# A two-block transformer forward pass: HGRN level products of two blocks at once, and a rearranged start

## The chip, the cores and the metric

The kernel runs on one core of a Trainium2 chip. The metric is the device time of one execution in microseconds (us), the median of several runs. Engines: TensorE (PE for its matmuls, PEld for its weight loads), VectorE (DVE), ScalarE (ACT), GpSimd (POOL) and SyncE (SP, which here only issues DMAs). They run side by side and meet at semaphores. Each takes its own instructions in order.

## The reference

One sequence of 512 tokens of width 1024 goes through two layers, in float32. The first has gated linear attention, dilated attention and a squared-relu MLP. The second has stick-breaking attention, an HGRN2 mixer and a gated MLP. The part of the HGRN mixer that the change touches:

```python
def hgrn2_mixer(q_in, f_in, i_in, g_in, lb, norm_g):
    f = lb + (1.0 - lb) * jax.nn.sigmoid(f_in)
    log_f = jnp.log(f)
    key = 1.0 - f
    q = jax.nn.silu(q_in)
    val = i_in
    ...
        b = jnp.cumsum(gc, axis=2)
        diff = b[:, :, :, None, :] - b[:, :, None, :, :]
        decay = jnp.exp(jnp.where(mask, diff, -jnp.inf))
        attn = jnp.einsum('bhtk,bhsk,bhtsk->bhts', qc, kc, decay)
        o_intra = jnp.einsum('bhts,bhsv->bhtv', attn, vc)
    ...
    o = rms_norm(o, norm_g)
    return o * jax.nn.silu(g_in)
```

And the first step of the first layer:

```python
nx = rmsnorm(h, attn_norm_g[l])
proj = jnp.einsum('bsd,dp->bsp', nx, w_in[l])
```

## The kernel before

**Products of activations with weights.** Activations lie transposed (features on the 128 partitions, 512 tokens along the row). Every weight matrix is cut into units of 8 k-steps by 256 columns, and a unit into pieces of at most 1024 columns. SP brings a piece to `RAW` (three buffers), ACT rounds it to its high part `WH` (five buffers), and its low part `WL` is the difference. For pieces 2 to 7 POOL makes `WL` (L1682), for pieces 0 and 1 DVE (L1093), and from piece 8 on (`ADDED`) ACT writes the negated high part (L734) and POOL issues a DMA that adds the weights to it (L1678). Activations have a high and a low part too (`NH`, `NL`), so every k-step of a tile is three matmuls of 512 columns: high by high (L432), low activation (L434), low weight (L436). The normalisation's factor is applied after the product, so the first products need only x times the norm's weights (`gains`): row k of `NH` on ACT (L707), of `NL` on DVE (L1098). The squares, their sum `acc` and the mean (L449, fp32, 512 columns) run beside them.

**The order.** Every engine's program is a merge of streams. Each stream yields a due time, and `merge` always takes the earliest. The unit of time is one k-step of a full tile, three matmuls. `T_H` is where the last projection of the second layer, `gs` (16 tiles), begins, and `h_time(i)` places task i of HGRN at `T_H + 0.1 + 3 (i + 2)`: three k-steps between two tasks.

**HGRN.** A head's 512 tokens are four blocks of 128. The causal products inside a block are done by levels, m = 1, 2, 4, ... 64: at level m the first half of each pair of stretches of m tokens holds keys, the second half queries. There are 8 tasks in each of 4 heads: task 0 is the diagonal (L605), tasks 1 to 7 the levels (L612). For a level:

1. DVE takes differences of cumulative log gates into `hD` (L1511, and L1513 for m under 64).
2. ACT takes the exponential (L960, or L946 and L948 for m = 64).
3. DVE multiplies with keys and queries into `hX` (L1493 and L1494, 256 elements each).
4. TensorE makes four products, one a block: a block's 128 columns of `hX` are the weights, its 64 query columns stream.
5. DVE stores the allowed entries into `ATh` with a mask (`keep_level`, L1285; the diagonal at L1543).

Two pairs of buffers (`hD`, `hX`) alternate. Blocks further apart have their own products of `x128` and `x256` (L620, L626). At the end of a head `sum_values` (L544) multiplies `ATh` with the values `vH`, and the result's mean of squares is a product with a matrix of 1/128 (L639).

DVE and ACT also serve the gates' products in this stage: the scaling out of PSUM (L1576) and the sigmoid (L675, L677, L679 on ACT, L683 on DVE, L687 on ACT).

## Time and profile before

| | us |
|---|---|
| median of 3 runs | 1421.49 |
| lowest and highest | 1420.95 and 1422.03 |
| the profiled execution's own time | 1421.15 |
| its span in the trace | 1419.9 |

| engine | busy, us | share of the span |
|---|---|---|
| PE | 1392.8 | 98% |
| PEld | 1129.2 | 80% |
| ACT | 864.4 | 61% |
| DVE | 619.5 | 44% |
| POOL | 203.3 | 14% |

Stages can be found by their lines. The first two tiles run from 7 to 23 us. The HGRN tasks run from 834 to 944 us. A matmul's busy time includes the drain of its pipeline, so its start to the next start tells the rate. An fp32 product appears as two rows of PE, one a pass. A timeline row with an "idle before" part names how long the engine stood and what ended that.

### The profile page before, as it was taken

How to read it: one execution, taken by the hardware profiler on the slowest of the kernel's cores; microseconds unless marked ns; L12 is line 12 of the kernel's file. 1: busy time of each engine (PE TensorE's matmuls, PEld its weight loads, DVE VectorE, ACT ScalarE, POOL GpSimd, SP SyncE). 2: the span in 40 equal slices, each digit the busy share in tenths (PEclk: the TensorE clock that was granted, in tenths of full speed). 3: DMA queues.
4: the chain of work that ended last, by engine and by line, in shares of the span. 5: the costliest groups of instructions: out<-in, count | busy, mean ns of one | idle time of the engine just before them, and what ended most of it. 6: DMA issues, size and time to landing. Idle time of an engine off the chain costs nothing.

```text
span 1419.9 us, 17692 instructions
## 1 busy us (share of the span) xinstructions
PE 1392.8 (98%) x6886; PEld 1129.2 (80%) x6886; DVE 619.5 (44%) x1177; ACT 864.4 (61%) x1267; POOL 203.3 (14%) x231
## 2 busy tenths in 40 slices
PE   7999999999999999999989999999999999999999
PEld 5977966788888888887867778887788888888887
DVE  5054466521211212357578778955534322341232
ACT  5574575654644535666678778676556644663562
POOL 3210000111111111111100011011111111111110
PEclk9999999999999999999999999999999999999999
DMA  6976543698888888877744566669988888888875
GB/s 216 240 166 144 142 114 90 153 209 192 193 191 199 194 188 198 191 169 169 166 109 105 119 144 149 162 149 267 223 200 188 196 188 199 190 194 192 195 168 125
DMA packets 72935, 247.93 MB, mean 175 GB/s; under 512 B 8242, under 2 KB 8258, under 8 KB 72724
## 3 DMA queue, kind: packets, MB, share of 16 engines
q0 software_dynamic: 31536, 113.54, 46.8%
q1 hardware_dynamic: 40452, 131.67, 27.7%
q10 hardware_dynamic: 864, 1.60, 0.3%
q8 instruction: 54, 0.88, 0.2%
q14 instruction: 29, 0.24, 0.1%
HBM read 240.45 MB, written 6.32 MB: 174 GB/s over the span
## 4 chain that ended last, share of the span: by engine, by line
PE 84%; ACT 7%; DVE 5%; issue 2%; DMA 2%; POOL 0%; DVEq 0%; ACTq 0%; POOLq 0%
PE bank L432 25%; PE bank L436 25%; PE bank L434 25%; PE bank L612 2%; ACT WH L726 1%; PE bank L544 1%; ACT WL L734 1%; DVE eb L1352 1%; DMA WL<-in_w_in 1%; ACT eb L880 1%; PE bank L563 1%; PE bank L587 1%; DMA RAW<-in_w_in 1%; PE bank L577 1%; DVE eb L1348 1%
## 5 line engine op out<-in xcount | busy, mean ns | idle before, releaser
L432 PE MATMUL bank<-NH,WH 128*128 128x512 f32 x1152 | 468.3, 407 | 8.6 <-ACT NH L707 7.0
L434 PE MATMUL bank<-NL,WH 128*128 128x512 f32 x1152 | 451.3, 392 | 1.0 <-DVE NL L1098 0.5
L436 PE MATMUL bank<-NH,WL 128*128 128x512 f32 x1152 | 451.1, 392 | 0.2 <-POOL WL L1682 0.2
L726 ACT ACTIVATE WH<-RAW 128x1024 fp32r<-128x1024 f32 (+2 forms) x227 | 235.2, 1037 | 210.3 <-PE bank L436 196.1
L432 PEld LDWEIGHTS bank<-NH,WH 128*128 128x128 f32 x1152 | 217.2, 189 | 73.4 <-issue 30.8
L434 PEld LDWEIGHTS bank<-NL,WH 128*128 128x128 f32 x1152 | 217.4, 189 | 48.9 <-issue 3.8
L436 PEld LDWEIGHTS bank<-NH,WL 128*128 128x128 f32 x1152 | 217.1, 188 | 46.7 <-POOL WL L1682 0.6
L734 ACT ACTIVATE WL<-WH 128x1024 fp32r<-128x1024 f32 (+2 forms) x219 | 229.6, 1048 | 5.6
L434 PE MATMUL bank<-AL,WH 128*128 128x512 f32 x432 | 168.2, 389 | 0.0
L436 PE MATMUL bank<-AH,WL 128*128 128x512 f32 x432 | 168.1, 389 | 0.0
L432 PE MATMUL bank<-AH,WH 128*128 128x512 f32 x432 | 168.0, 389 | 0.0
L1378 DVE TENSOR_TENSOR hT<-hT,bank 128x512 f32<-128x512 f32 x80 | 54.8, 686 | 221.6 <-PE bank L436 221.6
L1678 POOL DMA_DIRECT2D WL<-in_w_in x62 | 53.9, 880 | 405.6 <-ACT WL L734 400.8
L1678 POOL DMA_DIRECT2D WL<-in_w_ff x64 | 55.2, 863 | 298.6 <-ACT WL L734 298.6
L434 PEld LDWEIGHTS bank<-AL,WH 128*128 128x128 f32 x432 | 81.1, 188 | 17.3 <-DVE AL L1626 0.3
L436 PEld LDWEIGHTS bank<-AH,WL 128*128 128x128 f32 x432 | 81.1, 188 | 16.9
L432 PEld LDWEIGHTS bank<-AH,WH 128*128 128x128 f32 x432 | 81.1, 188 | 16.7
L432 PE MATMUL bank<-WH,NH 128*128 128x256 f32 (+1 forms) x256 | 76.1, 297 | 0.0
L436 PE MATMUL bank<-WL,NH 128*128 128x256 f32 (+1 forms) x256 | 72.6, 284 | 0.7 <-DMA WL<-in_w_in 0.7
L434 PE MATMUL bank<-WH,NL 128*128 128x256 f32 (+1 forms) x256 | 72.5, 283 | 0.0
L1678 POOL DMA_DIRECT2D WL<-in_w_gu x44 | 38.0, 864 | 202.3 <-ACT WL L734 202.3
L675 ACT ACTIVATE ft<-ft 128x512 f32<-128x512 f32 x22 | 13.9, 632 | 68.8 <-DVE ft L1609 68.8
(277 smaller groups left out, 1645.8 us busy)
## 6 DMA issues: line engine op xcount, KB each, us to landing
RAW<-in_w_in SPq DMA_DIRECT2D x64, 512.0 KB, 5.6
RAW<-in_w_ff SPq DMA_DIRECT2D x64, 512.0 KB, 6.3
WL<-in_w_ff POOLq DMA_DIRECT2D x64, 512.0 KB, 8.7
WL<-in_w_in POOLq DMA_DIRECT2D x62, 512.0 KB, 7.9
RAW<-in_w_gu SPq DMA_DIRECT2D x44, 512.0 KB, 6.3
WL<-in_w_gu POOLq DMA_DIRECT2D x44, 512.0 KB, 8.8
RAW<-in_w_down SPq DMA_DIRECT2D x20, 512.0 KB, 4.7
WL<-in_w_down POOLq DMA_DIRECT2D x20, 512.0 KB, 8.5
```

The costliest lines, as they stand in the source:

```text
L432: e.matmul(o, a[0], a[1], start=(k == 0), stop=False)
L434: e.matmul(o, b[0], b[1], start=False, stop=False)
L436: mm = e.matmul(o, c[0], c[1], start=False, stop=(k == t.kt - 1))
L544: mm = e.matmul(OB[:, t0:t0 + w], vs[:, j, h * P:(h + 1) * P], a[:, a0:a0 + w], start=(n == 0), stop=(n == len(seq) - 1), skip_group_check ...
L563: mm = e.matmul(OB[po:po + 64, i * P:(i + 1) * P], vs[:, j, h * 64:(h + 1) * 64], wbuf[p][:, j * P:(j + 1) * P], start=(j == 0), stop=(j = ...
L577: mm = e.transpose(bank[:, j * P:(j + 1) * P], z[:, j * P:(j + 1) * P], ident)
L587: e.matmul(FB[p][:, 0:n], qs[64 * p:64 * p + 64, hp, i * P:(i + 1) * P], ks[64 * p:64 * p + 64, hp, 0:n], start=True, stop=True).then_inc( ...
L612: mm = e.matmul(bank[:, j * 64:(j + 1) * 64].rearrange("p (n m) -> p n m", m=m), x[:, js], halves(x[:, js], m)[1], start=True, stop=True)
L726: e.activation(WH[p % HL][:, 0:n], RAW[p % RAWS][:, 0:n], ACT.Copy).then_inc(*act.sig("high", p))
L734: e.activation(WL[p % HL][:, 0:n], WH[p % HL][:, 0:n].bitcast(F32), ACT.Copy, scale=-1.0).then_inc(*act.sig("high_negated", p))
L1378: e.tensor_tensor(hT[:, k, :], hT[:, k, :], bank_for(t), ALU.add).then_inc(*dve.sig("evac_v", t.g))
L1678: e.dma_start(WL[p % HL][:, 0:n], src[:, k * cols:(k + m) * cols], accum_op=ALU.add).then_inc(*pool.sig(f"low_added{p % HL}", p, by=16))
```

## The change

**Level products.** Two blocks of 128 tokens now go through one product. Their 128 keys (64 of each block, the second block's in reversed order) are the weights' columns, and their 128 queries stream, so a level has two products with 128 columns in place of four with 64. Entries between blocks are not masked in. For this the keys part of `hX` is written as two instructions, the second reversed, and the queries part as one (`pair_values`). In the odd blocks the positions of the keys are reversed throughout: ACT makes the reversed keys `hkr` for the diagonal, the blocks 1 and 3 of `vH` are turned once by a product with a reversed identity (`turn`) and copied back by ACT, and the masks are laid out anew. `turn` takes the place of the 1/128 matrix, so the heads' means are made with 1/1024 and a scale of 8.

**Start.** The first two tiles are done side by side: k-step by k-step, each of the three matmuls for both tiles. The low parts of pieces 0 to 7 are all made by DVE. The norm weights come with x's first row in one transfer. DVE makes the first row of `NH`. Three products of zeros stand ahead of the first matmul. Piece 4 is split before the squares, the last four squares come later, and the mean is due at 24 instead of 14.

```diff
@@ class Plan
+                if u == 0 and c:
+                    first = self.together[0][0]
+                    t.v0, first.v1 = first.v0, v - 1
+                    self.together[0].append(t)
...
+    def order(self):
+        for tiles in self.together:
+            for k in range(tiles[0].kt):
+                for part in range(3):
+                    for t in tiles:
+                        yield t, k, part
...
+def pairs(x):
+    return x[:, 0:2 * P], x[:, 2 * P:4 * P]
...
-            return ("low_first" if p < 2 else "low" if p < ADDED else f"low_added{p % HL}", p)
+            return ("low_first" if p < ADDED else f"low_added{p % HL}", p)
...
-                return [-20.0, -18.4, -15.4, -13.4, 8.2][p]
-            return max(plan.used[p - HL], 8.3 + 0.01 * p) + 0.1
+                return [-20.0, -18.4, -15.4, -13.4, -11.5][p]
+            return plan.used[p - HL] + 0.1
...
+        def first_square(k):
+            return -10.0 + k if k < 4 else 4.2 + 0.1 * k
+
-        mean_time = {"attn": 14.0,
+        mean_time = {"attn": 24.0,
...
+            def early():
+                yield -50.0
+                pe.wait_ge(("zeros",))
+                for n in (S, S, UC):
+                    e.matmul(OB[:, 0:n], rs[:, 0:P], rs[:, 0:n], start=True, stop=True)
...
-                        pe.wait_ge(("gate", "hq", h), ("hk", h), *free)
+                        pe.wait_ge(("gate", "hq", h), ("hk", h), ("keys_turned", h), *free)
                         for j in range(NT):
                             js = slice(j * P, (j + 1) * P)
-                            mm = e.matmul(bank[:, js], hk[:, h, js], hq[:, h, js], start=True, stop=True)
+                            keys = hkr[:, j // 2 * P:(j // 2 + 1) * P] if j % 2 else hk[:, h, js]
+                            mm = e.matmul(bank[:, js], keys, hq[:, h, js], start=True, stop=True)
                     else:
-                        m = 1 << (n - 1)
-                        x = xx[(i - h - 1) % 2]
+                        y, z = pairs(xx[(i - h - 1) % 2])
                         pe.wait_ge(("hg_x", i, 1), *free)
-                        for j in range(NT):
-                            js = slice(j * P, (j + 1) * P)
-                            mm = e.matmul(bank[:, j * 64:(j + 1) * 64].rearrange("p (n m) -> p n m", m=m), x[:, js],
-                                          halves(x[:, js], m)[1], start=True, stop=True)
+                        for c in range(2):
+                            cs = slice(c * P, (c + 1) * P)
+                            mm = e.matmul(bank[:, cs], y[:, cs], z[:, cs], start=True, stop=True)
...
+            def turns():
+                yield T_H + 0.3
+                for j in (1, 3):
+                    bank, free = take("turn", j)
+                    pe.wait_ge(*evacuated("vH"), *free)
+                    e.matmul(bank, turn, vH[:, j, :], start=True, stop=True).then_inc(*pe.sig("turn", j))
...
-                e.dma_start(gv_, A["gains"]).then_inc(*act.sig("gains", by=16))
-                for i in range(0, 8, 2):
+                e.dma_start(first_in, A["xT"][:, 0:64 + S]).then_inc(*act.sig("x0", by=16))
+                at["gains",] = at["x0",]
+                for i in range(2, 8, 2):
...
+                def keys():
+                    for h in range(4):
+                        yield T_H + 0.6 if h == 0 else h_time(8 * h - 3, 1.2)
+                        act.wait_ge(("hk", h), *(stick_end if h == 0 else [("hg_prod", 8 * h - 8)]))
+                        odd = hk[:, h, :].rearrange("p (c w t) -> p c w t", c=2, w=2)[:, :, 1, ::-1]
+                        e.activation(hkr.rearrange("p (c t) -> p c t", c=2), odd, ACT.Copy).then_inc(*act.sig("keys_turned", h))
+
+                def turns():
+                    yield T_H + 1.5
+                    for j in (1, 3):
+                        act.wait_ge(("turn", j))
+                        e.activation(vH[:, j, :], bank_of("turn", j), ACT.Copy).then_inc(*act.sig("values_turned", j))
+                        give(("turn", j), ("values_turned", j))
...
+                yield -19.0
+                dve.wait_ge(("x0",))
+                e.tensor_scalar(NH[:, 0, :], hT[:, 0, :], g_attn[:, 0:1], None, ALU.mult).then_inc(*dve.sig("first_row"))
...
+                def pair_values(i, m, d, x, h):
+                    y, z = pairs(x)
+                    y = y.rearrange("p (c n h m) -> p c n h m", c=2, h=2, m=m)
+                    dv, kv = (a.rearrange("p (c w n h m) -> p c w n h m", c=2, w=2, h=2, m=m) for a in (d, hk[:, h, :]))
+                    dve.wait_ge(("hg_decay", i, 0) if m >= 64 else ("hg_decay", i, 1))
+                    e.tensor_tensor(y[:, :, :, 0, :], dv[:, :, 0, :, 0, :], kv[:, :, 0, :, 0, :], ALU.mult)
+                    e.tensor_tensor(y[:, :, ::-1, 1, ::-1], dv[:, :, 1, :, 0, :], kv[:, :, 1, :, 0, :],
+                                    ALU.mult).then_inc(*dve.sig("hg_x", i, 0))
+                    dve.wait_ge(("hg_decay", i, 1))
+                    e.tensor_tensor(z.rearrange("p (n m) -> p n m", m=m), halves(d, m)[1], halves(hq[:, h, :], m)[1],
+                                    ALU.mult).then_inc(*dve.sig("hg_x", i, 1))
...
+            def zeros():
+                yield -60.0
+                e.memset(rs, 0.0).then_inc(*pool.sig("zeros"))
```

The far values `x256` are written in three instructions in the same way, their second block reversed.

**TensorE, the first task and the first level of HGRN, before.** L605 is the diagonal, L612 a level:

```order
L605 MATMUL bank<-hq,hk 128x128 [waits dve_root,hk,gate]
L605 MATMUL bank<-hq,hk 128x128 x3
L432 MATMUL bank<-NH,WH_54 128x512
...
L612 MATMUL bank<-hX_138 128x64 [waits dve_root,hg_vector]
L612 MATMUL bank<-hX_138 128x64 x3
```

The same place now. L671 are the turned values, L643 the diagonal, L649 a level:

```order
L671 MATMUL bank<-vH,cf 128x512 [waits dve_root] x2
L466 MATMUL bank<-NH,WH_54 128x512
...
L643 MATMUL bank<-hq,hk 128x128 [waits keys_turned,dve_root,hk,gate]
L643 MATMUL bank<-hq,hkr 128x128
L643 MATMUL bank<-hq,hk 128x128
L643 MATMUL bank<-hq,hkr 128x128
L466 MATMUL bank<-NH,WH_55 128x512
...
L649 MATMUL bank<-hX_138 128x128 [waits dve_root,hg_vector]
L649 MATMUL bank<-hX_138 128x128
```

A level is two products in place of four; two products of 512 columns stand ahead of the diagonal, and the diagonal has one more signal to wait for.

**ACT at the start of the HGRN stage, before.** L960 is the first level's exponential, L734 the negated weights, L675 to L679 the sigmoid of the last hg tile:

```order
L960 ACTIVATE hD_136<-hD_136 128x512 [waits hg_vector]
L734 ACTIVATE WL_57<-WH_52 128x1024 [waits high]
L675 ACTIVATE hs_126<-mixed_114 128x512 [waits gate,evac_v]
L677 ACTIVATE hs_126<-hs_126 128x512 [waits sigmoid_a]
L679 ACTIVATE hs_126<-hs_126 128x512 [waits sigmoid_a]
```

Now:

```order
L1004 ACTIVATE hD_136<-hD_136 128x512 [waits hg_vector]
L1035 ACTIVATE hkr<-hk 128x256 [waits stick_out]
L1041 ACTIVATE vH<-bank 128x512 [waits turn] x2
L778 ACTIVATE WL_58<-WH_53 128x1024 [waits high]
L718 ACTIVATE hs_126<-mixed_114 128x512 [waits gate,evac_v]
L720 ACTIVATE hs_126<-hs_126 128x512 [waits sigmoid_a]
L722 ACTIVATE hs_126<-hs_126 128x512 [waits sigmoid_a]
```

The reversed keys and two copies out of PSUM stand between the exponential and the sigmoid.

**DVE at the first level, before and now.** L1493 and L1494 are the keys and the queries of a level, now L1571, L1572 and L1575:

```order
L1493 TENSOR_TENSOR hX_138<-hD_136,hk 128x256 [waits hg_decay,hk,gate]
L1494 TENSOR_TENSOR hX_138<-hD_136,hq 128x256
L1511 TENSOR_TENSOR hD_137<-hB 128x128x2
L1513 TENSOR_TENSOR hD_137<-hB 128x128x2
```

```order
L1571 TENSOR_TENSOR hX_138<-hD_136,hk 128x128 [waits hg_decay,hk,gate]
L1572 TENSOR_TENSOR hX_138<-hD_136,hk 128x2x64
L1575 TENSOR_TENSOR hX_138<-hD_136,hq 128x256
L1593 TENSOR_TENSOR hD_137<-hB 128x128x2
L1595 TENSOR_TENSOR hD_137<-hB 128x128x2
```

One instruction more a level, with the same number of elements.

## Rows read from the trace of the kernel before

**Rows 1.** The page's first part: busy time, share of the span, instructions.

```profile
PE 1392.8 (98%) x6886; PEld 1129.2 (80%) x6886; DVE 619.5 (44%) x1177; ACT 864.4 (61%) x1267; POOL 203.3 (14%) x231
```

**Rows 2.** Busy time by engine in two windows, HGRN's heads 0 and 1.

```profile
834.14:861.79 27.65, 25.65 (x145) 21.64 (x144) 23.79 (x56) 20.52 (x37) 2.59 (x3) 1.00 0.68 153
861.79:889.95 28.16, 28.16 (x162) 24.13 (x161) 24.71 (x56) 22.31 (x38) 3.45 (x4) 1.00 0.60 154
```

**Rows 3.** Waits of PE, whole span: total us, times, longest.

```profile
PE bank L612 <- DVE hX L1494: 1.2, 1, 1.2
PE bank L612 <- DVE ATh L1543: 0.8, 1, 0.8
```

**Rows 4.** Timeline of the start: start us, us, engine, line, [idle before <-releaser].

```profile
7.05 0.77 PE L432 MATMUL bank<-NH,WH 128*128 128x512 f32 x1 [7.05 <-ACT NH L707]
7.38 0.63 ACT L726 ACTIVATE WH<-RAW 128x512 fp32r<-128x512 f32 x1 [0.47 <-DMA RAW<-in_w_in]
```

**Rows 5.** Timeline of PE, 12 to 24 us.

```profile
12.61 0.62 PE L436 MATMUL bank<-NH,WL 128*128 128x512 f32 x1
13.04 0.44 PE L432 MATMUL bank<-NH,WH 128*128 128x512 f32 x1
...
20.46 0.39 PE L434 MATMUL bank<-NL,WH 128*128 128x512 f32 x1
20.69 0.39 PE L436 MATMUL bank<-NH,WL 128*128 128x512 f32 x1
...
21.03 1.10 PE L449 MATMUL bank<-acc,cf 128*128 128x512 f32 x2
...
23.44 0.50 PE L436 MATMUL bank<-NH,WL 128*128 128x512 f32 x1 [0.15 <-POOL WL L1682]
```

**Rows 6.** Timeline of PE, three HGRN tasks.

```profile
858.82 1.00 PE L612 MATMUL bank<-hX 128*128 128x64 f32 x8
...
861.79 1.05 PE L605 MATMUL bank<-hq,hk 128*128 128x128 f32 x8
...
864.77 1.00 PE L612 MATMUL bank<-hX 128*128 128x64 f32 x8
```

**Rows 7.** Timeline of PE, the far products of head 0.

```profile
840.15 0.61 PE L620 MATMUL bank<-hX 128*128 128x128 f32 x4
840.60 1.03 PE L626 MATMUL bank<-hX 128*128 128x256 f32 x4
```

**Rows 8.** Timeline of ACT at the start of the HGRN stage.

```profile
833.60 0.61 ACT L960 ACTIVATE hD<-hD 128x512 f32<-128x512 f32 x1
834.12 1.04 ACT L734 ACTIVATE WL<-WH 128x1024 fp32r<-128x1024 f32 x1
```

**Rows 9.** Groups of ACT, 838 to 945 us: busy us, mean ns | idle before.

```profile
L983 ACT ACTIVATE ATh<-bank 128x512 f32<-128x512 f32 x4 | 2.4, 600 | 0.0
...
L948 ACT ACTIVATE hD<-hD 128x256 f32<-128x256 f32 x4 | 1.6, 401 | 0.0
```

**Rows 10.** Timeline of DVE in the HGRN stage.

```profile
837.04 0.69 DVE L683 SCALAR_TENSOR_TENSOR hs<-mixed,hs 128x512 f32<-128x512 f32 x1 [2.91 <-ACT hs L679]
...
854.81 0.42 DVE L1493 TENSOR_TENSOR hX<-hD,hk 128x256 f32<-128x256 f32 x1 [0.96 <-ACT hD L960]
855.16 0.42 DVE L1494 TENSOR_TENSOR hX<-hD,hq 128x256 f32<-128x256 f32 x1
...
872.28 0.43 DVE L1493 TENSOR_TENSOR hX<-hD,hk 128x256 f32<-128x256 f32 x1 [1.39 <-PE bank L612]
```

**Rows 11.** Groups of DVE by shape, 838 to 945 us.

```profile
L1493 DVE TENSOR_TENSOR hX<-hD,hk 128x256 f32<-128x256 f32 x28 | 11.7, 418 | 10.9 <-PE bank L612 7.1 <-ACT hD L960 3.5
...
L683 DVE SCALAR_TENSOR_TENSOR hs<-gx,hs 128x512 f32<-128x512 f32 x12 | 8.2, 680 | 1.0 <-ACT hs L679 1.0
```

**Rows 12.** The two scans by line: ns min/median/max, first and last start, forms.

```profile
L1352 DVE TENSOR_TENSOR_SCAN eb<-eb x32: 397/808/1220, 697.0 to 814.6; 128x128 f32<-128x128 f32 x8, 128x256 f32<-128x256 f32 x8, 128x384 f32<-128x384 f32 x8, 128x512 f32<-128x512 f32 x8
...
L1461 DVE TENSOR_TENSOR_SCAN hB<-resets,hB x8: 1185/1208/1225, 820.4 to 902.5; 128x512 f32<-128x512 uint8 x8
```

196 lines of the change are left out of this document (106 added, 90 removed).

## The prediction, made before the changed kernel ran

> **What bounds the kernel now.** I read the page first, then the waits of TensorE, then its order of time in two stretches. Matmuls fill 98% of the span, 1392.8 of 1419.9 us [rows 1]. So an edit pays if it shortens work on TensorE or removes one of its few waits, as long as the engine that feeds it keeps up. The change touches two stretches, the first 30 us and the HGRN stage from 834 to 946 us; what it does elsewhere (the mean of a GLA head with 1/1024 and a scale of 8, other mask layouts, norm weights in another tile) issues the same instructions with the same shapes, and I cost it at nothing.
>
> In the HGRN stage TensorE works without a gap from 845 us on: a head takes 28.16 us and all of it is busy, DVE is busy 24.71 us of it and ACT 22.31 [rows 2]. Only at its start does it wait, 1.2 us for the first level's operands and 0.8 us for a store [rows 3].
>
> At the beginning the first matmul starts at 7.05 us, released by the operand row that ACT made [rows 4]. The next ones follow each other by 0.43 us (12.61 to 13.04), and by 0.23 us at 20.46 to 20.69 [rows 5]: the lower and the upper level of the clock, 1.2 and 2.4 GHz by the ratio, since 512 columns take 0.427 us at 1.2 GHz. The page's clock column says 1.00 throughout and does not show this. The mean's product comes at 21.03 us, after 45 of the 48 matmuls of the first two tiles. At 0.23 us these 45 need 10.3 us, and they took 13.9. So 3.6 us of the stretch are low clock and waits for operands, and then piece 4's low part, made late by POOL, shows up as a wait at 23.44 us, which with the gap ahead of it on the load side costs about 0.5 us [rows 5].
>
> **Term 1, the level products.** A level task now is four fp32 products of 64 columns (eight rows in the trace, two passes each). Task to task is 2.97 us (858.82 to 861.79), with nine products of 0.23 in between: 2.97 - 2.07 = 0.90 us for a task. The diagonal task has the same eight rows with 128 columns instead of 64 and takes the same, 864.77 - 861.79 - 2.07 = 0.91 [rows 6]. So neither is set by its columns; each row costs about 0.11 us, whichever of the two widths it has. Four rows of 128 columns stand at 840.15, and the next group begins at 840.60: 0.45 us [rows 7]. That is exactly the new form of a level task: half the rows, each twice as wide. The gain is 0.45 us a task, 28 tasks, 12.6 us of TensorE time.
>
> The Trainium skill (TensorE: Matmul & The Clock Gate, Step-by-step: what each phase is for) says that weight loads are pulled ahead of matmuls in flight and so are hidden. By that rule halving the loads would gain nothing, since passes times columns stay 512 in a task; the rows with 64 and with 128 columns speak against it here. That outcome is rival B below.
>
> **Term 2, what the stage pays for it.** TensorE gets two products of 512 columns (L671 of the new kernel, the reversed blocks 1 and 3 of vH) shortly after the start of the gates' products. The same shape, the mean's product at 21.03, is busy 1.10 us, of which the last 0.16 overlap the next one (a 0.39 us product follows at 0.23): 0.93 each, 1.9 us together [rows 5]. They come before the wait of 1.2 us for the first level [rows 3], which swallows most of that.
>
> ACT gets in its order, between an exponential and the negated weights, the reversed keys (256 elements) and two copies of 512 out of PSUM. One of 512 follows the last by 0.52 us (833.60 to 834.12) [rows 8]; a 256-element one is busy 0.40 against 0.60 for the 512 [rows 9], so 0.31 behind each other. Together 1.35 us. Queued behind them are the sigmoid's three steps of the last hg tile, and DVE waits exactly for that, 2.91 us, at 837.04 [rows 10]. So DVE's first level operands come 1.35 us later. Later heads have only the 0.31 us copy of the keys, on an engine with 5 us to spare in a head.
>
> DVE gets three instructions instead of two for a level's values, and for x256. 256 elements are busy 418 ns and 512 are busy 680 [rows 11], so an element costs 1.02 ns; 128 elements would be 287. An instruction starts before the last ends: 854.81 to 855.16 is 0.35 us for one of 0.42 [rows 10], an overlap of 0.07 to 0.08. Two of 128 against one of 256 are then 2 x 0.20 - 0.34 = 0.07 us more; 32 times, 2.2 us in the stage, 0.56 us in a head. The writes are reversed: the reversed scan of stick-breaking takes 1220 ns at most for 512, the forward one of HGRN 1208 [rows 12], so a negative step costs nothing; ACT reading the keys backwards has no row. I take no extra cost, and a quarter more on each of the two short ones (0.1 us a task) as the bad end.
>
> Head by head. **Head 0** (834.14 to 861.79) is set by DVE: it is busy 23.79 us of 27.65 [rows 2], nearly without a gap until 853, and TensorE waits already. The whole chain moves 1.35 us later and grows by 0.07 a task. Its operands for level task 6 were begun at 854.81 and ready at 855.16 + 0.42 [rows 10]; I get 857.3 for them. Task 7 then starts at 859.9 against 858.82, and the next head's first task at 862.4 against 861.79: a loss of 0.6 us in place of the 3 us gain. If the ACT copies fall into gaps, it gains up to 2.3; that is the good end. **Heads 1 and 2**: TensorE needs 28.16 - 3.15 = 25.0 us, DVE 24.7 + 0.56 = 25.3. Balanced to 1%, but DVE enters head 1 with operands more than 2 us ahead of use (its wait of 1.39 us at 872.28 is for a buffer that TensorE frees [rows 10]), and this lead lasts two heads: gain 3.1 each, and 2.5 each, less up to 1.2 of waits for ACT, where it does not last. **Head 3**: DVE prepares no further head (three scans and two differences fewer), so the full 3.1. Sum: -0.6 + 3 x 3.1 = 8.7 us, between 4.5 and 11.5.
>
> **Term 3, the first 30 us.** Removed: one DMA ahead of x's first row, one row on ACT (DVE makes it), and POOL's low parts (DVE makes them). Added: three products of zeros from about 1.5 us, whose 2.5 x 0.93 us at the upper clock are 4.3 us at the lower, so they end near 6, before the operands. The clock rose 6.0 us after the first matmul (7.05 to 13.04) [rows 4, 5]; counted from 1.5 us it is up at about 7.5. The first real product starts near 6.4. Then the operands set the pace: ACT's row order behind the second weight piece, which landed at 7.38 us [rows 4], is unchanged, so the second row of x is ready at 8.7 and its low part at 9.4. But a row is now used by six matmuls (1.37 us) and not three, and a new row comes each 0.7 us, so from row 2 on (10.4 us) nothing is waited for: 36 x 0.23 later, at 18.6, both tiles are done. Before, the 48th is done at 21.03 + 0.93 + 3 x 0.23 = 22.6, and 0.5 of waiting followed. The mean's 0.93 now comes later. The gain is 22.6 - 0.93 + 0.5 - 18.6 = 3.6. I take 0.3 off, since the mean (moved ten steps later) needs seven squares that now stand behind two wide splits on ACT, and behind four more low parts on DVE (1.1 us each for the wide ones by the 1.02 ns): 3.3 us. If the clock does not stay up over the gap between zeros and operands, the products up to 13 us take 0.43 each, partly inside waits that are there anyway; the two tiles then end near 20.3 and the gain is 1.8; that is the low end, 3.8 the high. What is late next is DVE: its low parts and sums fill it until 24 us, but the banks that wait for the scale come due only at step 32.
>
> **Sum.** 1421.15 us is the profiled execution's own time (span 1419.9), 0.34 under the median of 1421.49. 1421.15 - 8.7 - 3.3 = 1409.15, and with the 0.34 to the median 1409.5 us.
>
> **The rivals.** (A) DVE sets the pace of heads 1 and 2 too. For: 25.3 against 25.0 us; ACT waits for DVE and DVE for ACT there. Against: the lead. Gain 4.5 to 5.5 in the stage: 1421.5 - 5 - 3.3 = 1413.2. (B) The loads were hidden, halving them gains nothing: the stage loses 1.1 to 2 us by the turns and ACT's copies, the start still gains 3.3: 1419.7. Against it: 0.90 and 0.91 us for 64 and 128 columns. (C) The clock is not up when the operands come: 1421.5 - 8.7 - 1.8 = 1411.0. For: the gap after the zeros. (D) Slower than before: the reversed, four-level patterns make DVE's level values much dearer. One mechanism, in the three instructions of L1571 to L1575; it decides from (28.16 - 25.3) / 7 = 0.4 us a task on top of mine, where a head takes as long as before. At 0.9 us a task heads 1 to 3 lose 3.5 each and head 0 6, less 3.3: 1434.6. Against: the scan, and that 128x256 costs 418 ns in every pattern of levels 0 to 6 [rows 11]. (E) Better: head 0 isn't delayed and gains 2.3: 1406.6.
>
> **How the numbers follow.** Forecast 45%, A 22%, C 13%, E 12%, B 5%, D 3%. The first four lie between 1406 and 1414.5 us, with 92%; B and D are left out. A measurement of this kernel can tell about 0.2% from no change: faster by more than that (under 1418.6) 0.93, within it 0.05, slower 0.02.
>
> **What would show it.** Right: level tasks two rows each, 2.5 us apart; head 1 to head 2 near 25 us with no TensorE wait; first task of head 1 later than, or near, 861.79 less the gain of the start; spacing 0.23 before 9 us; mean's product near 24. Wrong: level tasks still 2.97 apart without waits (B), TensorE waits on DVE's hX in heads 1 and 2 (A), spacing 0.43 until 12 us (C), a 128x128 product on DVE over 0.35 us (D).

## The result, and the profile after

The changed kernel takes 1414.42 us, the median of 4 runs (1412.04 to 1414.91), against 1421.76 us (4 runs) for the kernel before on the same chip: ratio 0.9948, 95% interval 0.9932 to 0.9963. The gain is 7.3 us, where 12.0 were forecast. The profiled execution took 1414.06 us, with a span of 1412.4 us against 1419.9. Over a whole span the mean granted clock was 0.999 in the fastest of the four runs and 0.995 or 0.996 in the other three, which are 2.0 to 2.9 us slower.

The page's first part of the changed kernel, which answers to [rows 1]:

```profile
PE 1386.7 (98%) x6784; PEld 1119.7 (79%) x6784; DVE 624.8 (44%) x1216; ACT 865.4 (61%) x1272; POOL 192.7 (14%) x227
```

TensorE is still busy 98% of the span. It lost 102 recorded matmuls and 6.1 us of busy time.

**The level tasks are as forecast.** The timeline of TensorE in head 1 of the changed kernel, two level tasks and the product behind the first, beside [rows 6]:

```profile
869.74 0.61 PE L649 MATMUL bank<-hX 128*128 128x128 f32 x4
870.11 0.47 PE L466 MATMUL bank<-NH,WH 128*128 128x512 f32 x1
...
872.27 0.61 PE L649 MATMUL bank<-hX 128*128 128x128 f32 x4
```

Four rows of 128 columns, and 2.53 us from task to task instead of 2.97: less 2.07 for the nine products in between, a task costs 0.46 us. VectorE's two new products of 128 elements, from the timeline of VectorE:

```profile
880.64 0.29 DVE L1571 TENSOR_TENSOR hX<-hD,hk 128x128 f32<-128x128 f32 x1 [0.38 <-ACT hD L992]
880.85 0.29 DVE L1572 TENSOR_TENSOR hX<-hD,hk 128x128 f32<-128x128 f32 x1
881.05 0.42 DVE L1575 TENSOR_TENSOR hX<-hD,hq 128x256 f32<-128x256 f32 x1
```

Each is busy 0.29 us and they follow each other by 0.20 to 0.21, which is what the sum had; reversed writes into blocks cost nothing.

**But heads 1 and 2 gained only half.** Each head begins with its diagonal task. In this table (us, from the two timelines of TensorE) the last column is the branch stage's first product:

| | head 0 | head 1 | head 2 | head 3 | branch stage |
|---|---|---|---|---|---|
| before | 834.14 | 861.79 | 889.95 | 918.10 | 967.24 |
| after | 834.18 | 860.74 | 887.16 | 913.75 | 960.05 |
| length before | 27.65 | 28.16 | 28.15 | 49.14 | |
| length after | 26.56 | 26.42 | 26.59 | 46.30 | |

("head 3" runs to the branch stage.) Of the forecast 3.1 us each, heads 1 and 2 gave 1.74 and 1.56. The waits of TensorE between 826 and 965 us (us in total, times, longest), where [rows 3] had one wait for hX and one for ATh in the stage (those two are the stage's rows of a whole-span table, in which larger ones stand, as 8.3 us in six waits for ScalarE's `wT`). The four largest:

```profile
PE bank L649 <- DVE hn L707: 2.7, 2, 1.4
PE bank L649 <- DVE hX L1575: 1.6, 3, 0.8
PE bank L466 <- ACT NH L875: 1.1, 1, 1.1
PE bank L649 <- DVE ATh L1625: 0.9, 1, 0.9
```

The largest was not in the prediction. The last level task of a head takes the PSUM bank that held the mean of the head before, and VectorE frees that bank with the correction step of the root (`root_better`). The timelines of TensorE and VectorE at the end of head 1:

```profile
882.93 0.39 PE L473 MATMUL bank<-NH,WL 128*128 128x512 f32 x1
884.56 0.68 PE L649 MATMUL bank<-hX 128*128 128x128 f32 x4 [1.25 <-DVE hn L707]
```

```profile
879.58 0.68 DVE L703 TENSOR_TENSOR hn<-sq 128x512 f32<-128x512 f32 x1
...
883.39 0.42 DVE L1557 TENSOR_TENSOR hX<-acc,hq 128x256 f32<-128x256 f32 x1
883.73 0.68 DVE L707 SCALAR_TENSOR_TENSOR hn<-bank,hn 128x512 f32<-128x512 f32 x1
```

Here L707 stands behind the values of the next tasks on VectorE: the step before it ends at 880.26, and it starts at 883.73. TensorE, now faster, stands at the task by 883.3 and waits until 884.41. In the kernel before the same step was no earlier in relation to VectorE's work (3.7 us behind the end of its predecessor, now 3.5), but TensorE came later. The two timelines of the kernel before at that place:

```profile
885.78 0.68 DVE L664 SCALAR_TENSOR_TENSOR hn<-bank,hn 128x512 f32<-128x512 f32 x1
```

```profile
886.97 1.00 PE L612 MATMUL bank<-hX 128*128 128x64 f32 x8
```

The bank was free at 886.46, 0.5 us ahead of its use. A slack of 0.5 us does not show in a table of waits.

**Head 0 went as forecast.** It is 1.09 us shorter, but the two turned products ahead of it take away 1.77: an equal product ahead of the stage (`kS,qS` with 512 columns) starts at 804.69 us, 1.73 earlier than before (806.42), and the first diagonal task came 0.04 us later. That is -0.68 (forecast -0.6). VectorE at the start of the stage, where [rows 10] had 2.91 us of idle time ahead of the same instruction:

```profile
836.58 0.69 DVE L726 SCALAR_TENSOR_TENSOR hs<-mixed,hs 128x512 f32<-128x512 f32 x1 [4.18 <-ACT hs L722]
```

**At the start the clock came up, and fell again.** The timeline of TensorE, beside [rows 4, 5]:

```profile
1.31 4.44 PE L434 MATMUL bank<-rs 128*128 128x512 f32 x6 [1.31 <-POOL rs L1764]
7.34 0.70 PE L466 MATMUL bank<-NH,WH 128*128 128x512 f32 x2 [1.59 <-DVE NH L1143]
8.04 0.73 PE L470 MATMUL bank<-NL,WH 128*128 128x512 f32 x2
8.60 0.85 PE L473 MATMUL bank<-NH,WL 128*128 128x512 f32 x2
9.42 1.22 PE L466 MATMUL bank<-NH,WH 128*128 128x512 f32 x2
10.44 1.05 PE L470 MATMUL bank<-NL,WH 128*128 128x512 f32 x2
```

and the busy times in three windows (span; busy time of PE, PEld, DVE, ACT, POOL; granted clock; DMA share; GB/s):

```profile
7.60:9.40 1.80, 1.80 (x6) 0.68 (x5) 0.99 (x3) 1.28 (x3) 0.00 (x0) 0.84 1.05 405
9.40:12.10 2.70, 2.70 (x7) 2.06 (x7) 2.70 (x6) 2.70 (x5) 0.00 (x0) 0.50 1.01 392
12.10:20.40 8.30, 8.30 (x37) 6.81 (x36) 6.35 (x9) 5.93 (x10) 0.00 (x0) 0.99 0.81 268
```

The zeros end at 5.75. The first real product starts at 7.34 and not at 6.4, after an idle time of 1.59 us. The first pairs follow at 0.56 to 0.70 us, then (from 9.42 on) at 0.85 to 1.02 with a granted clock of 0.50 (1.2 of 2.4 GHz), and from 12.1 on at 0.46 to 0.52 again. The two tiles end at 20.40.

**Between the two stretches the trace lost 1.1 us again.** Between the start and the HGRN stage TensorE has the same work in both kernels. In stick-breaking it waits 3.6 us for ScalarE, in both. Its timeline at the end of this wait, before and after:

```profile
726.05 1.17 PE L563 MATMUL bank<-wT,vS 128*64 128x128 f32 x12 [3.59 <-ACT wT L865]
```

```profile
723.33 1.55 PE L600 MATMUL bank<-wT,vS 128*64 128x128 f32 x12 [3.58 <-ACT wT L909]
```

So here the changed kernel is 2.72 us ahead. Behind this wait the granted clock falls in both. The windows from there to the next `kS,qS` product with 512 columns, before, after, and in zeros_none (an experiment below):

```profile
726.05:745.59 19.54, 19.54 (x106) 13.88 (x106) 15.55 (x36) 17.54 (x37) 1.87 (x3) 0.91 0.55 135
723.33:743.96 20.63, 20.63 (x105) 15.01 (x105) 15.56 (x37) 17.64 (x37) 1.97 (x3) 0.86 0.53 128
723.50:742.42 18.92, 18.03 (x105) 12.90 (x105) 14.94 (x36) 16.92 (x35) 1.73 (x2) 1.00 0.57 133
```

The clock stayed low longer in the changed kernel's execution, and the stretch took 1.09 us more. In the 14 traces of this study it takes 18.92 to 20.63 us, and the clock falls in it in 13 of them. Kernels with the same instructions there differ by a microsecond (zeros_longer 19.58, act_copies_late 20.60), so this is not the change's doing; what sets the length of the fall is open. What the start gives is therefore read at 723 us, ahead of it, and not at the entry of the HGRN stage.

### The profile page after: what moved, and what is told of

Its sections match the earlier page's. It is cut to its first block, busy times and chain, and to the rows that moved or that the text cites. A ratio compares the mean times of both kernels' runs of the same rounds, so it can differ in the third digit from the quotient of the medians.

```text
span 1412.4 us, 17525 instructions
## 1 busy us (share of the span) xinstructions
PE 1386.7 (98%) x6784; PEld 1119.7 (79%) x6784; DVE 624.8 (44%) x1216; ACT 865.4 (61%) x1272; POOL 192.7 (14%) x227
## 4 chain that ended last, share of the span: by engine, by line
PE 78%; ACT 8%; DVE 8%; issue 3%; DMA 2%; SPq 0%; DVEq 0%; ACTq 0%
PE bank L466 24%; PE bank L470 24%; PE bank L473 24%; ACT WH L770 2%; ACT WL L778 1%; PE bank L581 1%; PE bank L600 1%; DVE eb L1416 1%; DMA RAW<-in_w_out 1%; PE bank L624 1%; PE bank L614 1%; ACT eb L924 1%; ACT hs L720 1%; DMA gates<-hs 1%; DVE eb L1412 0%
## 5 line engine op out<-in xcount | busy, mean ns | idle before, releaser
L1442 DVE TENSOR_TENSOR gains_hT<-gains_hT,bank 128x512 f32<-128x512 f32 x80 | 54.9, 686 | 221.6 <-PE bank L473 221.6
```

What stands on the lines that cost most here:

```text
L1442: e.tensor_tensor(hT[:, k, :], hT[:, k, :], bank_for(t), ALU.add).then_inc(*dve.sig("evac_v", t.g))
```

## The experiments

Each is an edit of the changed kernel, unless it says otherwise. The kernel before ran beside each on the same chip, with medians of 1421.25 to 1421.41 us in these four groups of runs.

**Two halves.** Undo the HGRN part, or the start's part (each a set of reversed pieces of the diff that stands further up, so their core alone is shown).

```diff
 levels_old
-                        y, z = pairs(xx[(i - h - 1) % 2])
+                        x = xx[(i - h - 1) % 2]   # 4 products of 64 columns; no turns(), no keys()
 start_old
-                early(), products(),
+                products(),      # one tile after the other, gains in a DMA of their own, POOL's low parts
```

> The changed kernel with its new start, but the HGRN stage as before: four products of 64 columns a level, no turned keys or values. My account of the two traces gives the start 1.7 us of the 7.5 us of span (the tasks' stage begins 1.7 us earlier), so this kernel takes about 1420.0 us, and its first HGRN task begins near 832.4. If the start is worth what I forecast (3.3 us), it takes 1418.4. If the whole gain of the change came from elsewhere than I think and the start is worth nothing, 1421.6.

Measured: 1418.91 us (10 runs, 1417.53 to 1420.63), ratio 0.9984 [0.9975, 0.9994]. The start alone gives 2.5 us by the medians. In the profiled execution, the fastest of the ten, the clock did not fall at the start; the product behind the 3.6 us wait came at 722.54 us (726.05 before) and the first HGRN task, the diagonal, at 830.62 us (834.14 before), both 3.5 us earlier. With the old levels heads 1 and 2 were 28.15 us long again.

> The changed kernel with the old start (tiles one after the other, POOL's low parts, no zeros, ACT's first row), HGRN as in the change. By the traces' account the stage gives 5.5 to 6 us net: about 1416 us. In the stage the waits of TensorE of 1.25 and 1.42 us on the last level of heads 1 and 2 stay, since nothing of the start causes them. Rival: the gains of the two parts don't add, because the waits depend on the weights' timing; then it is 1418 or more, or under 1414.

Measured: 1416.79 us (5 runs, 1416.21 to 1417.58), ratio 0.9967 [0.9954, 0.998]. HGRN's part alone gives 4.6 us, where 8.7 were forecast. With 2.5 for the start that makes 7.1, and the whole gave 7.3: the halves add, and the larger shortfall is in HGRN. Its heads were 26.51, 26.48 and 26.58 us long, and the wait for L707 stood in its table with the same 2.7 us.

**The bank of the mean.** VectorE's `root_better` of the HGRN mean, one place earlier in its order: in front of the values of the next task and of x128 and x256.

```diff
-                        yield h_time(8 * h + 14, 1.7)
+                        yield h_time(8 * h + 13, 1.72)
                         root_better(key, bank_of(*bank), hn[2], unit=8.0)
```

> The changed kernel, with the instruction that frees the PSUM bank of a head's mean (the second step of the root on DVE) moved ahead of the far values of the next head but one. Theory: the last level task of heads 1 and 2 waits for this bank (1.25 and 1.42 us), not for DVE's own load. Then both waits go and the heads take about 25.2 us: 2.5 us less, about 1411.9. Rival: DVE sets the pace of the stage (it is busy 58.1 of 60 us); then the wait only moves to the next operands of a level and the time stays within 0.5 us of 1414.4.

Measured: 1411.56 us (4 runs, 1411.48 to 1411.74), ratio 0.9929 [0.9915, 0.9944], 2.9 us under the changed kernel. On VectorE L707 now follows its predecessor (L703, at 878.42) directly, at 879.14. Its waits of TensorE from 826 to 965 us:

```profile
PE bank L649 <- DVE hX L1575: 2.6, 5, 0.8
PE bank L466 <- ACT NH L875: 1.6, 1, 1.6
```

The 2.7 us for L707 are gone. Diagonal tasks come at 833.01, 859.53, 884.43 and 910.32 us, the branch stage at 957.63. So head 1 takes 24.90 us (forecast for it: 25.0) and head 2 25.89. This settles the cause for head 1. In head 2 the edit took away a wait of 1.42 us and gave 0.70: a wait of 0.65 us for hX stands there instead. The median flatters it, though. From the first diagonal task to the branch stage the trace has 124.62 us against 125.87, a gain of 1.25: heads 1 and 2 give 2.2, and 1.0 of that is lost after 910 us, in 0.3 us of waiting for hX at 913.72 and in a wait for ScalarE's first row at the branch stage of 1.60 in place of 1.14; the rest of the 1.0 has no wait of its own in the table. (The wait at the branch stage is 0.71 to 1.38 us in traces with the same stage and without this edit.) Another 1.2 us lie ahead of the stage, which the edit doesn't touch: 1.0 of them is the clock's shorter fall behind 723 us (19.60 us for that stretch against 20.63). Its four runs had a granted clock of 0.997 and 0.998, between those of the changed kernel's.

**ScalarE's copies.** The two turned blocks of vH are taken out of PSUM later, behind the sigmoid that VectorE waits for.

```diff
                 def turns():
-                    yield T_H + 1.5
+                    yield T_H + 4.5
```

> ScalarE takes the two turned blocks of vH out of PSUM after the low parts and the sigmoid's three steps of the last hg tile, in a stretch where it idled 2.17 us, and not ahead of them. Theory (head 0 is set by VectorE, which waits 4.18 us for that sigmoid at 836.58): the sigmoid and VectorE's first level values come 1.04 us earlier, and head 0 with what follows ends 1.0 us earlier: median 1413.4. Rival (TensorE's bank, held longer, or ScalarE's exponentials set head 0): the wait shrinks on VectorE, but the first task of head 1 does not move, 1414.4.

Measured: 1411.79 us (4 runs, 1411.03 to 1413.06), ratio 0.9932 [0.9917, 0.9947]. The timeline of VectorE at the same instruction:

```profile
835.70 0.69 DVE L726 SCALAR_TENSOR_TENSOR hs<-mixed,hs 128x512 f32<-128x512 f32 x1 [3.21 <-ACT hs L722]
```

4.18 us of idle time have become 3.21, and head 0 takes 25.58 us in place of 26.56 (diagonal tasks at 834.26 and 859.84). These 0.98 us are the predicted 1.04. The later heads take 26.46 and 26.56 us, as before the edit, with the 2.7 us for L707 again. At equal clock (0.996, the two profiled executions, with 20.60 and 20.63 us for the stretch behind 723 us) 1413.06 stands against 1414.06: 1.0 us. The 2.6 us between the medians hold more than that; the granted clock was 0.998 or higher in three of its four runs, and in one of four of the changed kernel's.

**The zeros.** One product of zeros more, and none.

```diff
 zeros_longer
-                for n in (S, S, UC):
+                for n in (S, S, S, UC):
 zeros_none
-                early(), products(),
+                products(),
```

> The changed kernel with one more product of 512 columns of zeros, so that TensorE works until about 7.5 us and the idle gap of 1.6 us ahead of the first real product closes. Theory: the lower clock between about 9 and 12.1 us comes from this gap; without it the products run at 0.23 us from the first on and the two tiles end near 18.9 in place of 20.4: 1.3 us less than the change, and runs lie closer together. Rival: the clock's fall has another cause (heavier DMA, or the kind of work); then low rows stay, and the zeros only push the first product back by 0.2 us: 1414.6.

Measured: 1413.40 us (4 runs, 1412.00 to 1415.06), ratio 0.9943 [0.9928, 0.9957]. The timeline of TensorE, and a window:

```profile
1.31 6.10 PE L434 MATMUL bank<-rs 128*128 128x512 f32 x8 [1.31 <-POOL rs L1764]
7.61 0.70 PE L466 MATMUL bank<-NH,WH 128*128 128x512 f32 x2 [0.20 <-DVE NH L1143]
8.31 0.73 PE L470 MATMUL bank<-NL,WH 128*128 128x512 f32 x2
```

```profile
9.40:12.10 2.70, 2.45 (x10) 1.65 (x10) 2.70 (x5) 2.70 (x6) 0.00 (x0) 1.00 1.06 382
```

The gap is 0.20 us, the clock stays at 1.00, and 10 matmuls start between 9.4 and 12.1 in place of 7. The product behind the 3.6 us wait comes at 722.64 us, 0.69 earlier, although the first real product starts 0.27 later. That is what closing the gap gave in the trace, about half of the 1.3 us that were expected. The first diagonal task comes at 832.52, 1.66 us earlier, but 1.05 of that is the shorter fall behind 723 us. The spread between runs stayed (clocks of 0.999 and 0.996, two each), so it was not, or not only, this gap. In which places the clock of the other runs was lower can't be read, since only one execution of a kernel has a trace.

> No products of zeros at the start; all else as in the changed kernel. Theory (the zeros matter only by the clock): the first product starts at about 7.3 us as before, every product until about 13.3 us takes 0.43 us, as in the kernel before (7.05 to 13.04), the two tiles end near 21 us (20.4 in the changed kernel's profile, whose clock fell again) and the median is 0.5 to 1 us above the changed kernel's 1414.4, and 2 to 2.5 us above the one with longer zeros. Rival (the clock is up by itself, or the operands alone set the pace): no difference in the tiles' end or the median.

Measured: 1415.08 us (4 runs, 1413.73 to 1417.20), ratio 0.9956 [0.9941, 0.9971]. Pairs from the timeline of TensorE, and a window:

```profile
8.47 1.06 PE L470 MATMUL bank<-NL,WH 128*128 128x512 f32 x2
9.32 1.05 PE L473 MATMUL bank<-NH,WL 128*128 128x512 f32 x2
10.17 1.05 PE L466 MATMUL bank<-NH,WH 128*128 128x512 f32 x2
```

```profile
9.40:12.10 2.70, 2.70 (x8) 2.09 (x7) 2.70 (x5) 2.70 (x6) 0.00 (x0) 1.00 1.02 391
```

0.85 us a pair is the lower level, until about 11.9 us; the column says 1.00 for it, as in the kernel before. By the medians no zeros cost 0.7 us against the changed kernel's and 1.7 against the longer ones; at a clock of 0.999 it is 1413.73 and 1414.00 against 1412.04 and 1412.00, or 1.7 to 2.0 us. That comparison is not quite like with like, since the column leaves out the low rate at the start. The traces say less: the product behind the 3.6 us wait comes at 723.50 us without zeros, 723.33 in the changed kernel and 722.64 with the longer ones, so 0.2 and 0.9 us. In the profile of the changed kernel the zeros had bought next to nothing: its clock fell, and the mean's product came at 26.52 us, against 26.66 without zeros and 25.81 with the longer ones.

**The first row.** VectorE makes the first row of operands before the first low part.

```diff
-                yield -19.0
+                yield -19.97
                 dve.wait_ge(("x0",))
```

> VectorE makes the first row of x times the norm weight before the low part of the first weight piece, and not behind it. Theory (the first product waits for that row, 0.6 us behind the low part): the row is made at 6.1 us, the first product starts at 6.75 instead of 7.34, the gap after the zeros is 1.0 instead of 1.6 us, and 0.3 to 0.6 us are gained, more if the shorter gap keeps the clock up (up to 1.8). Rival: the product then waits for the weight piece's high part or for the low part instead, and nothing is gained.

Measured: 1412.23 us (4 runs, 1411.65 to 1413.05), ratio 0.9935 [0.992, 0.995]; at a clock of 0.999 three runs of 1411.65 to 1412.34, against 1412.04, so the order by itself is not shown to gain. The timeline of TensorE:

```profile
6.60 0.70 PE L466 MATMUL bank<-NH,WH 128*128 128x512 f32 x2 [1.09 <-DVE NH L1143]
7.77 0.77 PE L470 MATMUL bank<-NL,WH 128*128 128x512 f32 x2 [0.47 <-DVE NL L1160]
8.34 1.05 PE L473 MATMUL bank<-NH,WL 128*128 128x512 f32 x2
9.67 1.22 PE L466 MATMUL bank<-NH,WH 128*128 128x512 f32 x2 [0.28 <-ACT NH L751]
```

The first product comes 0.74 us earlier than in the changed kernel, but the second row's first product 0.25 us later (9.67 against 9.42): ScalarE makes that row behind the second weight piece, which it got at 8.37 us against 8.12. So the next row sets the pace, and after a gap of 1.09 us the clock fell just the same. At 723 us nothing is left of the gain (723.57 against 723.33).

**GpSimd's low parts.** Pieces 2 to 7 on GpSimd again.

```diff
                     if p < ADDED:
-                        continue
+                        e.tensor_tensor(WL[p % HL][:, 0:n], RAW[p % RAWS][:, 0:n], ...)   # on pool
```

> The low parts of weight pieces 2 to 7 are made by GpSimd again, as in the kernel before; all else as in the changed kernel. Theory: GpSimd needs 1.28 us for 512 columns and 2.5 for 1024 where VectorE needs 0.69 and 1.2, so with two tiles sharing a row the products that use piece 4 and later wait for their low part by 0.5 to 1.5 us in the stretch from 15 to 25 us; median 0.5 to 1.5 us above the changed kernel's 1414.4. Rival: the products are slower to ask for a piece than GpSimd is to make it, and nothing changes.

Measured: 1414.71 us (4 runs, 1412.56 to 1415.73), ratio 0.9951 [0.9937, 0.9964]: no difference from the changed kernel that these runs could show. GpSimd takes 1.4 us for 512 columns and 2.4 to 2.7 for 1024, but up to 30 us no product waits for it, and the mean's product comes at 26.46 us, as in the changed kernel (26.52). The waits that the theory put there do not exist. One stands further on, in the timeline of TensorE:

```profile
39.99 0.40 PE L473 MATMUL bank<-WL,NH 128*128 128x272 f32 x1 [1.72 <-DMA WL<-in_w_vg]
```

It is for a transfer that GpSimd issues itself, behind its low parts. At 723 us all of it is still there (725.18 us against 723.33, so 1.85). At the first diagonal task 0.9 us is left (835.06 against 834.18), because the clock's fall in between was shorter (19.39 us for that stretch against 20.63). So this part of the change is worth about 1.9 us in the trace, by GpSimd's queue and not by its speed. The medians, 0.3 us apart with runs of pool_lows spread over 3.2, neither show nor exclude it.

**Together.** Root earlier, copies later, zeros longer:

> The changed kernel with three edits: VectorE's root of a head's mean one place earlier (ahead of the values of the next head), the two copies of vH later on ScalarE, and the zeros one product longer. If each acts on a limit of its own, their gains add: 2.9 for the root, 1.0 for the zeros, 1.0 for the copies, so 1414.4 - 4.9 = 1409.5. Rival: the copies' 1.0 us comes to nothing because with the bank free heads 1 and 2 go by VectorE: 1410.5.

Measured: 1410.49 us (4 runs, 1410.41 to 1411.61), ratio 0.9924 [0.9908, 0.9941]. Heads take 25.61, 24.92 and 25.85 us, and the branch stage begins at 956.24. In the heads the edits add, 1.0 and 2.2 us. 1.6 us of waiting at the branch stage stay. The 1409.5 was missed by 1.0, which is about what the root's edit gives back there; no run separates the two.

```diff
 four_together: as three_together, with the first row first, zeros (S, S, S), and on ScalarE
+                    yield -18.45 if k == 1 else -19.0 + k
 five_together: as four_together, x's rows 4 and 6 issued later, and
+ mixed_split("mixed2", k, plan.start("br0") - (2.2 if k < 2 else 0.8) + 0.1 * k, ...)
 six_edits: as five_together without that last line, and on VectorE
+                    yield (-19.96, -18.4)[k] if k < 2 else -18.9 + k
```

> As three_together (root of the mean earlier, copies of vH later, zeros closed up to the operands), with the start's order changed: VectorE makes the first row times the norm weight before the first low part, ScalarE the second row before the second weight piece's high part (it waited 2.05 us for that piece with the row at hand), and the zeros end at about 6.6 us instead of 7.2. Theory (ScalarE's 0.63 us for the second row stands between the piece's landing and the seventh product): the first product starts at 6.6, the second row's products 0.6 us earlier at about 9.1 instead of 9.79, and the median is 1410.5 - 0.6 = 1409.9, if the gap after the zeros stays under 0.5 us and the clock up. Rival (the clock falls in the start's waits): up to 1.5 us more, 1411.4.

Measured: 1410.83 us (5 runs, 1410.70 to 1411.84), ratio 0.9927 [0.9914, 0.9941], no gain over three_together. The second row's high parts were used at 8.71 us, but then:

```profile
10.36 0.73 PE L470 MATMUL bank<-NL,WH 128*128 128x512 f32 x2 [1.03 <-DVE NL L1160]
```

VectorE made the row's low part behind the weight piece's; the mean's product came at 25.68 us as in zeros_longer (25.81).

> As four_together, with two more edits. ScalarE's queue issues rows 4 and 6 of x only after the first weight piece has been split (about 6 us), not at 1.6 to 2.6 us: by theory they compete with the second weight piece, which landed at 8.1 us against 7.4 in the kernel before, so that it lands 0.5 us earlier. And the first two rows of the branch stage's operands are split before ScalarE's last exponential of the gates: TensorE waited 1.6 us there for the first of them (0.5 us of ScalarE's order), so 0.5 us. Median 1409.9 - 1.0 = 1408.9. Rival: the piece lands no earlier and rows 4 and 6 arrive late, 0.5 us lost at the start, 1409.9.

Measured: 1410.93 us (5 runs, 1410.81 to 1412.65), ratio 0.993 [0.9917, 0.9942]. ScalarE got the second weight piece at 7.80 us and not at 8.29, so rows 4 and 6 of x had indeed slowed it (the first pieces, at 5.54 and 5.59, differ by 0.05), and the first diagonal task came 0.7 us earlier. At the branch stage the edit split one wait into two:

```profile
955.04 0.47 PE L466 MATMUL bank<-NH,WH 128*128 128x512 f32 x1 [1.08 <-ACT NH L877]
...
958.15 0.47 PE L466 MATMUL bank<-NH,WH 128*128 128x512 f32 x1 [1.04 <-ACT NH L877]
```

2.1 us in place of 1.6: the exponential that used to stand ahead of row 0 now stands ahead of row 2, and it waits 1.44 us for VectorE, whose part of the same gate got behind the low parts of rows 0 and 1. What the start gained, the branch stage lost.

> As five_together without its edit of the branch stage, and with VectorE's low parts of rows 0 and 1 of x ahead of the low parts of weight pieces 0 and 1. In four_together and five_together TensorE waited 0.3 to 1.0 us at the second product of each of these rows for exactly these two (rows' low parts at 6.85 and 9.08 behind weight parts of 0.6 us). Theory: both waits shrink by about 0.5 us, the mean's product comes at 24.2 to 24.7 instead of 25.7 us, and the median is 1410.5 - 1.0 = 1409.5. Rival: the sums' operands for the mean or the later weight pieces then set the pace, and the median stays within 0.3 us of 1410.8.

Measured: 1408.87 us (5 runs, 1408.52 to 1409.76), ratio 0.9913 [0.9899, 0.9926], the fastest kernel of the study, 5.6 us under the changed one. It has the start of five_together with one more edit, and not its edit at the branch stage. Its timeline of TensorE:

```profile
6.61 0.70 PE L466 MATMUL bank<-NH,WH 128*128 128x512 f32 x2 [0.17 <-DVE NH L1145]
7.30 0.73 PE L470 MATMUL bank<-NL,WH 128*128 128x512 f32 x2
7.90 0.73 PE L473 MATMUL bank<-NH,WL 128*128 128x512 f32 x2
8.48 0.62 PE L466 MATMUL bank<-NH,WH 128*128 128x512 f32 x2
8.94 0.62 PE L470 MATMUL bank<-NL,WH 128*128 128x512 f32 x2
```

No wait over 0.2 us after the first product, the second row's products at 8.48 (9.42 in the changed kernel, 9.79 in three_together), and the mean's product at 24.18 us. That is where the prediction had put it for the change itself ("near 24").

## Why the prediction was right in part, point by point

The range held the median of 1414.42 us, with its upper end of 1414.5: by 0.1 us, and two of the four runs lie above it. The forecast was 4.9 us too fast. In the trace 7.2 us are gained up to the branch stage: 2.7 by 723 us, less 1.0 from there to the HGRN stage, and 5.5 in it, where 3.3 was forecast for the start and 8.7 for the stage.

- **What bounds the kernel: right.** Work taken off TensorE came back as time wherever its feeders kept up. What the reading left out is that TensorE's lack of waits in head 1 [rows 2, 3] says nothing of how much slack its feeders had.
- **Term 1, 0.45 us a level task: right.** 2.53 us from task to task and four rows each, measured. Each row cost 0.11 us again, with 128 columns, and half the loads and matmuls with the same number of columns in all saved half the time. Rival B is dead. With it goes the reading that the prediction gave to the Trainium skill (TensorE: Matmul & The Clock Gate, Step-by-step: what each phase is for): the section says that loads are pulled ahead of matmuls in flight, and does not say that a load costs nothing where the matmul is too short to cover it. The change halves loads and matmuls together, so which of the two sets the 0.11 us is not shown. Four rows of 256 columns took about 0.86 us in the kernel before (840.60 to 841.69, less 0.23 for the product between), which makes 0.21 a row. By this estimate the columns set the time from 128 on, and doubling them once more would gain nothing.
- **VectorE's extra: right.** 0.29 us for 128 elements, 0.20 apart. Rival D is dead by the same rows.
- **Term 2, head 0: right,** -0.68 for -0.6, by the cause named: ScalarE's copies delayed the sigmoid, and VectorE waited 4.18 us, 1.27 more than before. act_copies_late took 0.97 of it back. That edit makes the condition of rival E true, but not its price: head 0 with the turned products then gains 0.3 us against the kernel before (25.58 + 1.77 against 27.65), not 2.3.
- **Term 2, heads 1 and 2: wrong.** The step that failed is "gain 3.1 each" with the lead of VectorE as its only condition. 1.74 and 1.56 were measured, 2.9 us less, and 2.7 of that are the two waits for the bank (1.25 and 1.42 us). The lead of the operands held; what came late was a bank. It lay in the rotation of four banks, and in VectorE's order behind work that was not urgent. mean_bank_early removed that wait, and head 1 took 24.90 us. So in head 1 it was not rival A, though it looks like it in the time: 1413.2 was given for A, for a limit by VectorE's throughput. VectorE's busy time in head 1 is close to the 25.3 us of the forecast, as a window of the changed kernel shows (its third number of busy time is VectorE's):

```profile
860.70:887.20 26.50, 25.25 (x134) 20.96 (x133) 25.50 (x66) 23.44 (x40) 3.45 (x4) 1.00 0.61 148
```

And head 2 in mean_bank_early stayed at 25.89 us with a wait of 0.65 us for hX: the lead did not last through two heads once the bank was out of the way, and A in small stands right behind it.
- **Term 2, head 3: nearly right.** 2.84 us for 3.1, with 0.43 us more of waiting for ScalarE at the branch stage, which had no term. TensorE arrives there earlier, ScalarE does not. This wait is the unsteady part: in the seven traces with the new levels and the root in its old place it is 0.71 to 1.38 us, and without it head 3 takes 45.16 to 45.19 us in all of them (48.43 before), a gain of 3.3.
- **Term 2 as a sum:** 8.7 forecast, 5.5 by the trace of the changed kernel, 4.6 by start_old's median.
- **Term 3, the start: the size was off.** 3.3 us were forecast, and the median of levels_old has 2.5. In the traces, TensorE's products `mixed,rel` behind the mean's come at 29.35 us in the kernel before, 27.47 in the changed one and 26.66 in levels_old, where the clock stayed up: gains of 1.9 and 2.7 us. By 723 us they are 2.7 and 3.5. The 0.8 between had no term: the kernel before waits 0.68 us at 52.11 us for the transfer of a low part, and the other two do not. So the agreement of 3.5 with 3.3 is luck; what the sum describes gave 2.7 even with the clock up. Two steps failed. The first is "The first real product starts near 6.4": it was 7.34, because the first weight piece reached ScalarE at 5.44 us instead of 4.75 and VectorE made the piece's low part (0.61 us) first. The first transfer of x is larger by the norm weights and issued 0.4 us earlier, beside that piece's; that this delays it is argued, no run takes it alone. With the clock up the two tiles ended at 19.6 (levels_old) and not at 18.6. The second is "it is up at about 7.5", taken as if it stayed up. It fell after the gap of 1.59 us, which was rival C: its "two tiles then end near 20.3" was measured as 20.40, and its gain of 1.8 as 1.9. So C's mechanism is shown in the trace of the changed kernel. It does not hold in each execution: in levels_old the same zeros and a gap of 1.55 us left the clock at 1.00 from 7.6 to 20.4 us.
- **The 0.5 us at 23.44, "made late by POOL" [rows 5]: right that it went, wrong on what removed it.** pool_lows has GpSimd's low parts back, and the wait does not return.
- **The rivals.** What happened is C at the start and a loss nearly of A's size in the heads, by another mechanism. Both together had no case of their own: A was 3.7 us and C 1.5 above the forecast, and 1409.5 + 3.7 + 1.5 = 1414.7, where 1414.4 was measured. That is close partly by luck, since the wait that went at 52.11 us and the longer fall behind 723 us stand in neither and nearly cancel in the trace. Two rivals that do not exclude each other needed their sum as a third, and it would have lain outside the range.

## What to carry to other kernels

Before you credit a shorter step on the bounding engine with its full length, look for what that engine will reach too early. Not only operands: for each PSUM bank in the rotation, find the instruction that frees it and how far ahead of the next use it ends (here 0.5 us, against 3 us of gain in a head). An instruction that frees a bank belongs in front of work on its engine that nobody waits for yet; here one changed due time removed 2.7 us of waits. And small edits at the start paid little one by one, since each moved the wait to the next operand. By the product at 723 us four_together gained nothing over three_together, five_together 0.7 us (lost again at the branch stage) and six_edits 1.7, of which 1.6 show in the medians.

## What was not expected of the hardware

- **The clock can fall again after it has risen on zeros.** After 4.4 us of zeros and 1.59 us of idle time the products ran at a granted clock of 0.50 from 9.4 to 12.1 us. With gaps of 0.17 to 0.51 us or none it stayed at 1.00 in the traces (zeros_longer, three_together, four_together, five_together, six_edits). With 1.55 us it stayed once (levels_old), with 1.09 to 2.45 us it fell in row_first, act_copies_late, pool_lows, mean_bank_early and the changed kernel. A gap of 1.03 us ahead of the fifth pair (four_together, 10.36 us) left it at 1.00. Far from the start, after the wait of 3.6 us at about 723 us, it fell in 13 of 14 traces.
- **The clock column misses the low rate at the very start.** In zeros_none it says 1.00 for 9.4 to 12.1 us while pairs take 0.85 us; in the changed kernel, where the rate had been high before, it says 0.50 for pairs of the same length. At a start, read the spacing.
- **A transfer moved ahead makes another late.** The first weight piece was used at 5.44 us instead of 4.75, the second at 8.12 instead of 7.38, with the DMA engines moving 405 GB/s (401 before) from 7.6 to 9.4 us. In the twelve traces with the new start the first piece is used at 5.44 to 5.79 us, in the two with the old start at 4.58 and 4.75. Taking two later rows of x out of the way brought the second back to 7.80.
- **Runs of one kernel differ by 2 to 3 us with the mean granted clock (0.999 or 0.996).** Single edits worth 1 us could only be told by the lengths of stretches in the trace. Some of them repeat within 0.1 us (head 0 without the copies' edit: 26.56, 26.52, 26.47, 26.59). Others do not: the 20 us behind 723 us differ by 1.7, head 3 up to the branch stage by 0.7. Take the difference between two points that have none of these in between.
